# A float32 transformer chain on one core: products for the modulation columns, TensorE's warming products, and the order around the latent attention

## What is computed

```
c_act = silu(c)
mod = c_act @ ada_w[l] + ada_b[l]
sh_m, sc_m, g_m, sh_f, sc_f, g_f = split(mod, 6)
h = rmsnorm(x, g0) * (1 + sc_m) + sh_m
# latent attention
c_kv = rmsnorm(kv_a[..., :256])
k_pe = rope(kv_a[..., 256:])
kv = c_kv @ kv_b_w                  # k_nope and v of 8 heads
q = rmsnorm(h @ q_a_w) @ q_b_w      # q_nope and q_pe
s = q_nope @ k_nope + q_pe @ k_pe   # masked, softmax
y = (softmax(s) @ v) @ o_w
x = x + g_m * rmsnorm(y, g1)
h = rmsnorm(x, g2) * (1 + sc_f) + sh_f
y = square(relu(h @ w_up)) @ w_down
x = x + g_f * rmsnorm(y, g3)
```

## Time and profile before

| | us |
|---|---|
| median of 3 executions | 1856.46 |
| lowest, highest | 1856.10, 1863.97 |
| the profiled execution | 1864.76 |
| its span, first to last instruction | 1863.0 |
| TensorE busy | 1803.8 |
| VectorE busy | 1088.5 |
| ScalarE busy | 604.3 |

### The profile page before, as it was taken

One profiled execution on the slowest core, in us unless ns is written; L12 is line 12 of the kernel. 1 busy time (PEld: TensorE's weight loads), 2 busy tenths in 40 slices (PEclk: granted clock), 3 DMA queues, 4 the chain that ended last, 5 costly groups with the idle time before them and its releaser, 6 DMA issues. The chain is left out here.

```text
span 1863.0 us, 22762 instructions
## 1 busy us (share of the span) xinstructions
PE 1803.8 (97%) x8102; PEld 1436.8 (77%) x8102; DVE 1088.5 (58%) x1564; ACT 604.3 (32%) x933; POOL 79.7 (4%) x132
## 2 busy tenths in 40 slices
PE   9998999999999999999999999999988999999996
PEld 8766777888888878886888888877755688888885
DVE  5655555655555666776556565667674665434354
ACT  4125544322222333223423232334243341323230
POOL 0000000000000000101000000010000100000001
PEclk9999999999999999998999999989999999999998
DMA  6221112454444414542255454412221224233221
GB/s 220 80 92 35 46 46 63 152 166 150 146 156 155 143 55 158 187 163 68 93 190 180 170 186 175 135 46 90 91 91 57 80 91 165 84 102 99 93 79 45
DMA packets 59983, 215.32 MB, mean 116 GB/s; under 512 B 6656, under 2 KB 6656, under 8 KB 59776
## 3 DMA queue, kind: packets, MB, share of 16 engines
q1 hardware_dynamic: 43632, 154.95, 24.6%
q0 software_dynamic: 16128, 58.73, 10.1%
q10 hardware_dynamic: 144, 0.59, 0.1%
HBM read 212.15 MB, written 2.10 MB: 115 GB/s over the span
## 5 line engine op out<-in xcount | busy, mean ns | idle before, releaser
L697 ACT ACTIVATE w_hi<-w_raw 128x1024 fp32r<-128x1024 f32 x285 | 300.0, 1055 | 494.0 <-PE psum L1544 430.1
L1542 PE MATMUL psum<-h_hi,w_hi 128*128 128x512 f32 x1072 | 418.5, 390 | 0.5 <-DVE h_lo L1024 0.5
L1543 PE MATMUL psum<-h_lo,w_hi 128*128 128x512 f32 x1072 | 417.8, 390 | 0.0
L1544 PE MATMUL psum<-h_hi,w_lo 128*128 128x512 f32 x1072 | 417.8, 390 | 0.0
L993 DVE TENSOR_TENSOR w_lo<-w_raw,w_hi 128x1024 fp32r<-128x1024 f32 x285 | 348.1, 1221 | 105.0 <-ACT w_hi L697 95.1
L1544 PE MATMUL psum<-hid_hi,w_lo 128*128 128x512 f32 x760 | 295.6, 389 | 0.0
L1542 PE MATMUL psum<-hid_hi,w_hi 128*128 128x512 f32 x760 | 295.6, 389 | 0.0
L1543 PE MATMUL psum<-hid_lo,w_hi 128*128 128x512 f32 x760 | 295.6, 389 | 0.0
L1542 PEld LDWEIGHTS psum<-h_hi,w_hi 128*128 128x128 f32 x1072 | 201.7, 188 | 43.1 <-DVE h_lo L1024 0.9
L1544 PEld LDWEIGHTS psum<-h_hi,w_lo 128*128 128x128 f32 x1072 | 201.7, 188 | 42.2
L1543 PEld LDWEIGHTS psum<-h_lo,w_hi 128*128 128x128 f32 x1072 | 201.5, 188 | 42.1 <-issue 0.2
(11 more groups left out here) (261 smaller groups left out, 1947.6 us busy)
## 6 DMA issues: line engine op xcount, KB each, us to landing
w_raw<-in_wstream SPq DMA_DIRECT2D x285, 512.0 KB, 3.6
ada_raw<-in_ada POOLq DMA_DIRECT2D x112, 512.0 KB, 3.8
x<-in_xT SPq DMA_DIRECT2D x8, 256.0 KB, 6.5
outT<-x SPq DMA_DIRECT2D x8, 256.0 KB, 2.1
con<-in_consts SPq DMA_DIRECT2D x1, 1028.0 KB, 10.4
con<-in_rope ACTq DMA_DIRECT2D x1, 576.0 KB, 3.9
par<-in_params SPq DMA_DIRECT2D x1, 259.0 KB, 3.0
```

The costliest lines, as they stand in the source:

```text
L697: act.activation(w_hi[:, slot, :], w_raw[:, slot, :], ACT.Copy).then_inc(whi_done, 1)
L1542: pe.matmul(bank, w_hi[:, slot, w], hi[:, ra + k, :], start=k == 0, stop=False)
L1543: pe.matmul(bank, w_hi[:, slot, w], lo[:, ra + k, :], start=False, stop=False)
L1544: mm = pe.matmul(bank, w_lo[:, slot, w], hi[:, ra + k, :], start=False, stop=k == nk - 1)
```

## The change

1. The sums of a modulation group are made by products with a tile of 128x128 that holds 1/128, not with a column of ones. Each writes 128 equal columns; the next one overwrites all but the first. "take" multiplies by 128 in the instruction that adds ada_b. The column of ones goes.
2. `modulation` gets a count of warming products that follow its groups. The four transitions get 2 and 4, 11 and 7, 5 and 4, 11 and 15. The nine behind transition 4's squares go.
3. K's blocks are "late": VectorE splits the weights after it has emptied the banks, not before. The rotation of k_pe lies between the two blocks, not ahead of them.
4. V's banks are emptied by ScalarE, with the same scale. It signals v_stored; VectorE waits for that and hands the bank back.
5. The rotation of the queries comes after three query blocks, not after four.
6. The 24 weighted rows: 8 with K's and the queries' blocks, 8 in attention (one per odd unit), 8 in the output projection.

```diff
@@ close, the plan
-        modulation(groups - 1)
+        modulation(groups - 1, warm[0])
...
-        if more:
-            modulation(more)
+        modulation(more, warm[1])
@@ the latent part of the plan
+    gemm("scaled", 1, "ckv", ckv, nk=2, nout=4, dst="proj", dst_at=0, rooted=counts["rstd"], late=True, rows=1)
     rope((20,), pe_at)
-    gemm("scaled", 2, "ckv", ckv, nk=2, nout=4, dst="proj", dst_at=0, rooted=counts["rstd"])
+    gemm("scaled", 1, "ckv", ckv, nk=2, nout=4, dst="proj", dst_at=4, rooted=counts["rstd"], late=True, rows=1)
...
+    gemm("scaled", 2, "q_a", q_a, dst_at=16, rows=2, **about)
     rotary = counts["o"]
-    gemm("scaled", 2, "q_a", q_a, nk=3, nout=2, dst="proj", dst_at=8, root="q_a", scale=192 ** -0.5,
-         rooted=counts["rstd"])
+    gemm("scaled", 1, "q_a", q_a, dst_at=8, rows=1, **about)
     rope((16, 17, 18, 19), rotary)
-    gemm("scaled", 2, "q_a", q_a, nk=3, nout=2, dst="proj", dst_at=12, root="q_a", scale=192 ** -0.5,
-         rooted=counts["rstd"])
+    gemm("scaled", 3, "q_a", q_a, dst_at=10, rows=3, **about)
...
-    add("attn", dict(hi=8, rhs=8, ada=24))
-    gemm("acc", 8, "h", mix, dst="y", first=True, sq=True, kouter=AHEAD)
-    close(3, "r_m1", ("g_f1",), 0)
+    add("attn", dict(hi=8, rhs=8, ada=8))
+    gemm("acc", 8, "h", mix, dst="y", first=True, sq=True, kouter=AHEAD, rows=8)
+    close(3, "r_m1", ("g_f1",), 0, (11, 15))
@@ ScalarE, values2
+                    for u in range(8):
+                        t, half = divmod(u, 2)
+                        o = s["at"]["o"] + u
+                        act.wait_ge(out_done, o + 1)
+                        act.activation(v_mla[:, t, half * S:(half + 1) * S], psum[:, o % BANKS, :], ACT.Copy,
+                                       scale=rcol[:, t:t + 1]).then_inc(v_stored, 1)
@@ VectorE, values2
-                        dve.wait_ge(out_done, o + 1)
-                        dve.tensor_scalar(v_mla[:, t, half * S:(half + 1) * S], psum[:, o % BANKS, :], rcol[:, t:t + 1],
-                                          None, ALU.mult).then_inc(bank_free, 1)
+                        dve.wait_ge(v_stored, u + 1)
+                        dve.sem_inc(bank_free, 1)
@@ VectorE, attention
-                        weighted(s["at"]["ada"] + i * 24 // UNITS, s["at"]["ada"] + (i + 1) * 24 // UNITS)
+                        weighted(s["at"]["ada"] + i // 2, s["at"]["ada"] + (i + 1) // 2)
@@ TensorE, mod
-                            mm = pe.matmul(psum[:, O_BANK, c:c + 1], acc_of(g)[:, m * P:(m + 1) * P],
-                                           ones_col[:, :], start=True, stop=True)
+                            mm = pe.matmul(psum[:, O_BANK, c:c + P], acc_of(g)[:, m * P:(m + 1) * P],
+                                           mean[128][:, :], start=True, stop=True)
                         mm.then_inc(acc_free, 1)
+                    keep_warm(s["warm"])
```

More of the change, by code:

```diff
@@ L133, in rope, with modulation, close @@
         add("rope", dict(rope=len(tiles)), tiles=tiles, stored_by=stored_by)
-    def modulation(groups):
-        add("mod", dict(mod=groups), groups=groups)
+    def modulation(groups, warm=0):
+        add("mod", dict(mod=groups), groups=groups, warm=warm)
     def gains(*names):
         add("gains", dict(gains=len(names)), names=names)
-    def close(groups, gain, names, more, wide=True):
+    def close(groups, gain, names, more, warm, wide=True):
         modulation(1)
         total()
-        modulation(groups - 1)
+        modulation(groups - 1, warm[0])
         rstd(EPS2 if wide else EPS1, wide=wide)
@@ L225, in make_plan @@
         gemm("acc", 8, "hid", hid, nk=nk, dst="x", first=False, sq=g == 2, rows=(12, 12, 0)[g])
-    close(5, None, ("g_m0",), 3, wide=False)
+    close(5, None, ("g_m0",), 3, (2, 4), wide=False)
     h = norm("h", gain="g_m0", shift=0)
@@ L265, in make_plan @@
     add("values2", dict(n=2, o=8), r0=ckv)
-    gemm("scaled", 2, "q_a", q_a, nk=3, nout=2, dst="proj", dst_at=16, root="q_a", scale=192 ** -0.5,
-         rooted=counts["rstd"])
+    about = dict(nk=3, nout=2, dst="proj", root="q_a", scale=192 ** -0.5, rooted=counts["rstd"])
+    gemm("scaled", 2, "q_a", q_a, dst_at=16, rows=2, **about)
     rotary = counts["o"]
-    gemm("scaled", 2, "q_a", q_a, nk=3, nout=2, dst="proj", dst_at=8, root="q_a", scale=192 ** -0.5,
-         rooted=counts["rstd"])
+    gemm("scaled", 1, "q_a", q_a, dst_at=8, rows=1, **about)
     rope((16, 17, 18, 19), rotary)
-    gemm("scaled", 2, "q_a", q_a, nk=3, nout=2, dst="proj", dst_at=12, root="q_a", scale=192 ** -0.5,
-         rooted=counts["rstd"])
+    gemm("scaled", 3, "q_a", q_a, dst_at=10, rows=3, **about)
     mix = counts["rhs"]
-    add("attn", dict(hi=8, rhs=8, ada=24))
-    gemm("acc", 8, "h", mix, dst="y", first=True, sq=True, kouter=AHEAD)
-    close(3, "r_m1", ("g_f1",), 0)
+    add("attn", dict(hi=8, rhs=8, ada=8))
+    gemm("acc", 8, "h", mix, dst="y", first=True, sq=True, kouter=AHEAD, rows=8)
+    close(3, "r_m1", ("g_f1",), 0, (11, 15))
     h = norm("h", gain="g_f1", shift=88)
@@ L1070, in step @@
                                or isinstance(t.b, int) and t.b < s.get("presplit", 0))
-                    if not nothing:
+                    if not nothing and not s.get("late"):
                         split_lo(t.n + AHEAD, (t.n0 + AHEAD) % SPLIT)
@@ L1101, in step @@
                             put(s, i, psum[:, (t.o0 + q) % BANKS, :], stored(s["dst"], i))
+                        if s.get("late"):
+                            split_lo(t.n + AHEAD, (t.n0 + AHEAD) % SPLIT)
                     elif evac == "rise":
@@ L1812, in _ @@
                     sum_squares(s)
-                    if PLAN[idx + 3]["kind"] != "mod":
-                        keep_warm(WARM)
                 elif kind == "total":
@@ L1821, in _ @@
                       .then_inc(aux_done, 1)
-                    keep_warm(WARM if idx + 2 < len(PLAN) and PLAN[idx + 1].get("groups", 0) < 2 else 0)
+                    keep_warm(0 if "groups" in PLAN[idx + 1] else WARM)
                 elif kind == "mod":
```

17 lines of the change are left out of this document (7 added, 10 removed).

## The result

| us | before | after |
|---|---|---|
| median (lowest to highest, executions) | 1860.22 (1856.1 to 1865.47, 4) | 1839.28 (1837.63 to 1839.95, 4) |
| profiled execution, its span | 1864.76, 1863.0 | 1839.95, 1838.1 |
| mean granted clock of that execution | 0.979 | 0.993 |

The ratio on record is 0.9871, with a 95% interval of 0.9849 to 0.9892, so the gain is clear of the noise. It is not the quotient of the two medians above, which is 0.9887: it fits a before of 1863.3, which is the median of the 40 executions of before that ran beside the experiments. The forecast was 1839. The four executions of before are the three that stood ahead of the prediction and one more of 1865.47 us, so their median is no longer 1856.46.

What follows compares the result with a forecast made beforehand. TensorE, busy in 97% of the span, was taken as the bound, with eleven half-clock stretches to win from. Terms 15.5 + 5.1 + 2.8 = 23.4 us took 1864.76 to 1841.4, set at 1839 for the median; range 1831 to 1850.

Steps and rivals of the forecast that it cites:

- The clock in the transitions: Four transitions and last feed-forward: wide and warming products keep TensorE at full clock, 15.5 us less in sum.
- One sign: Transitions: the squares were to take 6.9 to 7.3 us if the forecast held.
- The price of a wide product: Modulation products: each widened one costs 0 to 0.01 us more, 1 us at most over 112; taken as 0.
- rival of a floor for narrow products: Modulation products: wide ones 31 ns over in each of 224 instructions, 6.9 us come back, 1846; chance 0.03.
- K's banks: Latent part: four copies come ahead of rotation and split, the 3.64 us stop and halved stretch go, 5.9 us less.
- V by ScalarE: Latent part: ScalarE's eight copies, 0.60 to 0.75 us each, are hidden; 0 us gained, up to 1 lost.
- The queries' blocks: Query blocks to attention: earlier rotations on VectorE make TensorE wait 3.0 us, not 2.18; 0.8 us lost.
- Attention: Attention's turn waits: one weighted row ahead in VectorE's queue, not two; 0.75 x 3 + 0.52 = 2.8 us less.
- From profile to median: Whole kernel: 1841.4 by terms from the profiled execution, 1838.7 if the median run lacks part of the gain; 1839 taken.
- Warming in already halved transitions: Rival, transitions: 15 to 21 warming products at 0.43 us each overrun their gaps, slower at 1876; chance 0.03.
- the transitions' clock did fall in part: Rival, transitions: if half of them still fall, about 9 us stay, 1848; chance 0.16.
- late for the second K block: Rival, latent part: VectorE's copies of second K block or query blocks 2 us later each, clock halves again, 1846; chance 0.11.

Runs made afterwards that it cites:

- e1: Kernel before with the wide modulation products alone, no added warming products, latent part as before: 1848.45 us, ratio 0.9927.
- e2: Kernel before with the warming products in the four transitions alone, modulation products still one column wide: 1850.80 us, ratio 0.9934.
- e10: Changed kernel without added warming products and with modulation products of 16 columns in place of 128: 1844.58 us, ratio 0.9931.
- e9: Changed kernel without the added warming products in the transitions (nine stay in transition 4's last root): 1839.19 us, ratio 0.9872.
- e5: Changed kernel with V's eight banks emptied by VectorE again: 1838.17 us, ratio 0.9871.
- e6: Changed kernel with all 24 weighted rows back in attention: 1839.24 us, ratio 0.9875.
- e4: Kernel before with the edits to the latent part and attention alone (changes 3 to 6): 1849.99 us, ratio 0.9930.
- e3: Kernel before with wide modulation products and warming products together, latent part and attention as before: 1847.27 us, ratio 0.9920.
- e7: Changed kernel with eight more warming products at each of eight places in the four transitions, 64 in all: 1849.26 us, ratio 0.9930.
- e8: Changed kernel with warming products in attention, nine ahead of its first scores and eight ahead of each of the last two turns: 1834.68 us, ratio 0.9850.
- e11: e8 with eight weighted rows moved from the latent part to the output projection, and two warming products ahead of attention, not nine: 1839.09 us, ratio 0.9879.
- e12: e8 without the added warming products in the transitions (nine stay in the last root): 1836.72 us, ratio 0.9867.

## Why the prediction was right

**The clock in the transitions.** Held, in all of them, and in the last feed-forward. 14.6 us against a sum of 15.5: transitions 1 and 2, with their next stages, within 0.3 each, the third 2.8 for 3.1, the fourth 1.75 for 1.9. The evidence for it was one gap with 128-column products. e1, e2 and e10 now separate the causes. Width without warming is enough for the gain. Warming without width gave 8.5 of the 14.6 us, 1.6 of them in the last feed-forward, where it adds no product; in transitions 1 and 3 the clock fell in the one-column products that run ahead of the added ones. 16 columns lose the clock in two transitions and in the last feed-forward where e9 kept it. So the added warming products gave nothing in the transitions that the medians show. The 0.2 us that two of them were to cost in transition 1 came (16.16 us against e9's 15.94). I had thought that waits of 2.90 us would still need them; that was wrong, they only sometimes do. One sign was off: I wanted the squares in 6.9 to 7.3 us, and they took 7.03 in transition 1 and 7.5 in the others, with warming and without (7.54 and 7.55 in e1).

**The price of a wide product.** I took 0 to 0.01 us more each. 24 one-column instructions took 2.73 us, 24 of 16 columns 2.75, 24 of 128 columns 2.84: 0.005 us more an instruction, 1.0 us over all 224. The rival of a floor for narrow products fell. The Trainium skill, "TensorE: Matmul & The Clock Gate", section "Back-to-back issue gap", has about 60 against 134 cycles for a product by itself. The same section says that in a stream of weight loads and products both set the spacing, so the 6.9 us that the prediction worked out from the table, and did not believe, were never due; in this float32 stream the three widths differ by 4%.

**K's banks.** 5.6 us for 5.9; the first copy starts where the rotation started before (24.2 us behind the latent q's first product, against 24.0), and TensorE follows in 0.8. The wait left in the K blocks is 0.52 us.

**V by ScalarE.** 0 as forecast, within 0.3 us, at 0.69 us a copy: V's stage took 11.31 us before, 11.10 in after and 11.37 in e5.

**The queries' blocks.** I gave them 0.8 us of loss, with a wait of 3.0. The wait was 2.16 and the loss 0.2: VectorE's 9.0 us of work took 8.4 (1323.13 to 1331.54). That term was too dark. e6 shows what the rows cost there: without them the queries' blocks took 1.6 us less.

**Attention.** The mis-sized term: 2.8 forecast, 4.69 measured. The turn waits shrank by 0.85, 0.59, 0.85 and 0.52, which is the 2.8 to the letter. The other 1.9 us came from the halved stretch at attention's start, which I had left as it was. It was 3.4 us long in place of 6.8. The profiles price both: with before's waits and no such stretch attention took 75.00 (e6), so the long one cost 2.7; with after's waits and none 72.24 (e4), so the short one cost 0.75; the difference is the 1.9. e5's profile lacks the stretch though that part of its code is the same, and e1's lacks it with before's code there, so this is an execution's chance and not the change's merit.

**From profile to median.** By terms I had 1841.4 for the profiled execution and 1839.95 came. The 2.4 us off for the median's sake gave 1839, and the median was 1839.28. The reason for it holds in part: over the 40 executions of the kernel before, the time follows the mean granted clock (1854.01 us at 0.985, 1867.12 at 0.977, correlation -0.99), so they do differ by how long the clock is down. But only 10 of the 40 are under 1860, while two of the three that I had were: beside the experiments, medians of 7 to 12 executions of before lie from 1863.07 to 1863.83. Measured against those the change is worth some 24 us, nearly all of the profile's 24.9. So I started from a median 7 us too low and, by the discount, forecast a gain 6.7 us too small (17.5 in place of 24.2). That these two misses cancel to 0.3 us is luck; the sum by terms, 23.4 for the profile's 24.9, is what the prediction earned, and 1.9 of that is chance in attention.

**The rivals.** Warming in already halved transitions never came, since the clock was up ahead of each. With wide products the transitions' clock did fall in part in one profile (e9, no warming), for 1.5 us, not 9. VectorE was not late for the second K block.

**The parts add up, once chance is taken out.** In the profiles e3 gains 15.0 and e4 12.9, the change 24.9. Of the 3.0 us between, 2.4 lie at the start of the kernel, where e4's and e3's executions were ahead of before by 2.0 and 0.4 and after's was not, and 0.9 in attention.

## What to carry to other kernels

Where TensorE bounds a kernel and its clock falls, look at what it ran ahead of the fall, not only at how long it waited: in this kernel one-column products between stages cost as much time as 128-column ones and let the clock go, so try widening them first. Then put warming products only into waits that the timeline shows, counted to fit, since one too many costs up to its full 0.23 us (64 cost 10), and judge by medians with the clock beside them: they paid in attention (4.6 us) and not measurably in the transitions. Before moving work off a chain, read what lies ahead of the last item in the queue it goes to: eight rows were free in the output projection (with transition 4 it took 61.95 us with them, 61.94 without), sixteen made the stretch 5.4 us longer. And take the base from many executions: three gave a median 7 us too low.

## What the runs showed of the hardware

**Behind products with few columns the clock fell with no wait at all.** e2's transition 1 is the clearest place: 1.00 until 665.2, 0.52 from 665.7, in the middle of 32 one-column instructions that run from 662.91 to 667.5. In the first block of the kernel before, TensorE's timeline and a window, 20 instructions of eight columns run without a gap until 101.5, full-width ones follow at once, and then the clock halves. No run changes the width there, so it is not shown that the eight columns are the cause:

```profile
99.15 2.40 PE L1852 MATMUL psum<-log_f,con 128*128 128x8 f32 x20
...
102.00:106.00 4.00, 4.00 (x12) 0.57 0.39 113
```

**Whether a given gap costs the clock differs between executions of the same instructions.** That stretch is there in the profiles of before, after, e1, e3, e7, e8, e11 and e12 and not in those of e2, e4, e5, e6, e9 and e10, though no kernel touches the place. It lasts 3.4 us, so it costs about 1.7. The changed kernel may vary less: 1837.63 to 1839.95 in four executions, and 1837.18 to 1840.59 in six of e9, where before spans 1854.01 to 1867.12 in 40.
